# High weights first in a slab, low weights behind their own wait

## What is computed

```python
for i in range(2):                       # first model
    h = rmsnorm(x) ; proj = h @ w_in[i]  # attention, convolution and a state-space branch
    x = x + merged @ w_mix_o[i]
    gt, up = split(rmsnorm(x) @ w_ffn_in[i])
    x = x + (silu(gt) * up) @ w_ffn_out[i]
for l in range(2):                       # second model
    h = h + (sig(g1) * (yr @ ret_out[l]) + sig(g2) * (ys @ ssd_out[l])) @ w_o[l]
    h = h + (silu(gate) * up) @ w_down[l]
```

## Time and profile before

| | us |
|---|---|
| median of 3 runs (2136.08 to 2138.23) | 2136.47 |
| the profiled execution, its own time | 2139.59 |
| its span, first to last instruction | 2137.8 |
| PE busy | 2113.5 (99%) |
| DVE busy | 1640.1 (77%) |
| ACT busy | 1195.2 (56%) |

### The profile page before, as it was taken

How to read it: one execution, slowest core, us unless ns; L and a number is a source line. 1 busy time by engine, 2 the same in 40 slices (tenths; PEclk the granted TensorE clock), 3 DMA queues, 4 the chain that set the end, 5 groups by cost and what they waited for, 6 DMA issues and landing times.

```text
span 2137.8 us, 47790 instructions
## 1 busy us (share of the span) xinstructions
PE 2113.5 (99%) x18652; PEld 2055.5 (96%) x18652; DVE 1640.1 (77%) x2620; ACT 1195.2 (56%) x1803; POOL 58.5 (3%) x54
## 2 busy tenths in 40 slices
PE   9999999999999999999999999999999999999998
PEld 8999999999999999899999999999899999999998
DVE  8987877987877776778957877776678947877764
ACT  6646644565555445546648745445446658845443
POOL 0000000000000000000002200000000002200000
PEclk9999999999999999999999999999999999999999
DMA  7434655654446556554455566556554556565553
GB/s 251 159 128 141 204 190 186 195 171 142 151 157 215 190 189 206 187 168 158 161 190 191 167 203 208 186 187 213 185 169 148 169 183 193 174 201 186 187 189 127
DMA packets 109984, 385.00 MB, mean 180 GB/s; under 512 B 12480, under 2 KB 16768, under 8 KB 109312
## 3 DMA queue, kind: packets, MB, share of 16 engines
q1 hardware_dynamic: 101664, 368.66, 52.2%
q10 hardware_dynamic: 8160, 14.04, 2.1%
HBM read 381.53 MB, written 1.11 MB: 179 GB/s over the span
## 4 chain that ended last, share of the span: by engine, by line
PE 89%; DVE 6%; ACT 2%; issue 2%; DMA 0%; DVEq 0%; ACTq 0%
PE acc L777 25%; PE acc L779 24%; PE acc L778 24%; DVE w_lo L1811 2%; PE acc L896 1%; PE acc L897 1%; PE acc L898 1%; PE acc L841 1%; PE acc L843 1%; PE acc L842 1%; ACT w_hi L1310 1%; PE mid L1133 1%; PE mid L1214 1%; DVE pr L2564 0%; PE mid L964 0%
## 5 line engine op out<-in xcount | busy, mean ns | idle before, releaser
L1811 DVE TENSOR_TENSOR w_lo<-w_raw,w_hi 128x1024 fp32r<-128x1024 f32 x694 | 848.5, 1227 | 306.8 <-ACT w_hi L1310 297.9
L1310 ACT CAST w_hi<-w_raw 128x1024 fp32r<-128x1024 f32 x694 | 724.7, 1047 | 541.3 <-PE acc L779 473.5
L777 PE MATMUL acc<-h_hi,w_hi 128*128 128x256 f32 x2096 | 599.4, 286 | 0.3 <-DVE w_lo L1811 0.3
L779 PE MATMUL acc<-h_hi,w_lo 128*128 128x256 f32 x2096 | 587.5, 280 | 0.0
L778 PE MATMUL acc<-h_lo,w_hi 128*128 128x256 f32 x2096 | 586.3, 280 | 0.0
L777 PE MATMUL acc<-g_hi,w_hi 128*128 128x256 f32 x1456 | 410.0, 282 | 0.8 <-DVE w_lo L1811 0.7
L779 PE MATMUL acc<-g_hi,w_lo 128*128 128x256 f32 x1456 | 407.2, 280 | 0.0
L778 PE MATMUL acc<-g_lo,w_hi 128*128 128x256 f32 x1456 | 406.8, 279 | 0.0
L777 PEld LDWEIGHTS acc<-h_hi,w_hi 128*128 128x128 f32 x2096 | 395.7, 189 | 7.7 <-issue 5.7
L779 PEld LDWEIGHTS acc<-h_hi,w_lo 128*128 128x128 f32 x2096 | 396.1, 189 | 0.0
L778 PEld LDWEIGHTS acc<-h_lo,w_hi 128*128 128x128 f32 x2096 | 395.1, 188 | 0.5
(11 more groups left out here) (434 smaller groups left out, 3394.3 us busy)
## 6 DMA issues: line engine op xcount, KB each, us to landing
w_raw<-weights_d SPq DMA_DIRECT2D x695, 512.0 KB, 3.9
even<-rows_d ACTq DMA_DIRECT2D x16, 256.0 KB, 4.3
odd<-rows_d ACTq DMA_DIRECT2D x32, 128.0 KB, 3.4
p<-p_d ACTq DMA_DIRECT2D x3, 1080.0 KB, 8.5
rdec<-decay_d ACTq DMA_DIRECT2D x2, 768.0 KB, 5.3
p<-p_d SPq DMA_DIRECT2D x1, 1024.0 KB, 10.7
out_d<-work SPq DMA_DIRECT2D x4, 256.0 KB, 2.3
x_all<-x_d SPq DMA_DIRECT2D x1, 516.0 KB, 4.3
```

The source lines that it names most:

```text
L777: mm(dst, wh, hi[:, k, :], start=first and j == 0, stop=False)
L779: done = mm(dst, wl, hi[:, k, :], start=False, stop=last and j == len(ks) - 1)
L1310: nc.scalar.copy(w_hi[:, slot, :], w_raw[:, slot, :]).then_inc(hi_done, 1)
L1811: tt(w_lo[:, slot, :], w_raw[:, slot, :], w_hi[:, slot, :].bitcast(F32), SUB).then_inc(lo_v, 1)
```

## The change

`products` no longer makes the three matmuls of a block in turn. It first waits for ScalarE's cast (`hi_done`), does the two matmuls with the high weights for each k, then waits for VectorE's subtraction (`lo_v`), and does the eight matmuls with the low weights one after the other. The calls of `weights_of` in `slab_k8` and `slabs_long` go. The matmuls are the same and as many, and the waits `need` stay with the first loop.

```diff
                 slot = i % RING
+                pe.wait_ge(hi_done, at.slab + (i + 1))
                 for j, k in enumerate(ks):
                     if need is not None:
                         need(k)
-                    a = j * width + col
-                    wh, wl = w_hi[:, slot, a:a + P], w_lo[:, slot, a:a + P]
+                    wh = w_hi[:, slot, j * width + col:j * width + col + P]
                     mm(dst, wh, hi[:, k, :], start=first and j == 0, stop=False)
                     mm(dst, wh, lo[:, k, :], start=False, stop=False)
+                pe.wait_ge(lo_v, at.slab + (i + 1))
+                for j, k in enumerate(ks):
+                    wl = w_lo[:, slot, j * width + col:j * width + col + P]
                     done = mm(dst, wl, hi[:, k, :], start=False, stop=last and j == len(ks) - 1)
                 return done
...
             def slab_k8(at, i, t, need=None, hi=h_hi, lo=h_lo):
 
-                weights_of(at, i)
                 bank(at, t)
...
                         last_mean(0)
-                    weights_of(at, i + m)
                     ks = range(m * KD, min(m * KD + KD, blocks))
```

## The result

The changed kernel takes 2146.55 us (median of 5 runs, 2145.23 to 2148.08), the kernel before 2136.47: a ratio of 1.0043, with a 95% interval of 1.0032 to 1.0054. It is slower by 7 to 12 us. The forecast was 2147.7.

What follows compares the result with a forecast made beforehand. TensorE, busy 99%, was taken as the bound. The profiled 2139.6 us, -2.0 for waits and +13.2 for pace, gave 2150.8; the median lying 3.1 lower made it 2147.7 us, range 2132 to 2158.

Steps and rivals of the forecast that it cites:

- What bounds the kernel: TensorE, busy 99% of the span; one nanosecond in the matmuls' pace is 14.7 us, all low-weight waits a few us.
- The waits that go: Slab starts that waited for VectorE's subtraction now need the cast alone; pauses vanish, -4.1 us.
- The second `issue` at `r`: First slab on `r`: a pause listed under "issue" goes, 0.41 us, with the other layer's 0.8 us.
- The restart after a pause: Second matmul after a pause comes 0.20 us behind the first, not 0.12; some eight pauses gone give 0.6 us.
- The waits that grow: Slabs with late activations have more matmuls behind the last wait: `s` +1.5 us, `m` +0.6 us, `f` nothing.
- The pace: In `products`, eight low-weight matmuls in a row go slower than three in turn's 117.3 ns; the sixteen high ones keep it.
- The term of +13.2 us: Low-weight matmuls in `products`: 2.7 ns more for each of 4896 matmuls.
- The 120 ns: Pace of eight matmuls of high weights with `g_lo` ending `slab_raw`, taken for the eight low-weight matmuls in `products`.
- Rival 1: Order leaves the pace at 117.3 ns and waits alone decide: 2134.5 us, not slower; chance 0.38.
- Rival 2: Eight low-weight matmuls in a row go at 115 ns, as the 512-column rows: 2123 us, half of it 2129; chance 0.10.
- Rival 3: The sixteen high-weight matmuls slow to 118.1 ns too: 7.8 us more, 2155.5 us; shares the forecast's chance of 0.52.
- Rival 4: Low weights late by more than 1.88 us stop TensorE at the new mid-slab wait; given no chance of its own.

Runs made afterwards that it cites:

- e_three_rows: The changed kernel with three rows of eight matmuls per slab, and one common wait for eight matmuls of `slab_raw`; 2153.0 us, ratio 1.0060 to 1.0091.
- e_order: The changed kernel's matmul order, but with the old wait for `lo_v` in front of each slab and none in the middle; 2146.0 us, ratio 1.0027 to 1.0055.
- e_few: The kernel before with the changed order in only ten slabs, those whose low weights came late; 2137.1 us, ratio 0.9999.

## Why the prediction was right, and where it wasn't

**What bounds the kernel: right.** The pace of `products` decided. All waits together moved the time by less than a microsecond (-3.2 + 0.4 + 1.3 + 0.8 = -0.7), the pace by 8 to 9 (8.2 in the steps above; 14.7 ns x 612 slabs = 9.0). The total came nearer than its parts, and that is in part luck: the forecast had +11.2 us, the medians differ by 10.1, but pace and waits by the trace give 7.5 to 8.3. The pace was forecast 4 to 5 us too dear, the waits 1.3 us too cheap.

**The waits that go: -4.1 forecast, -3.2 measured, and 0.4 taken back.** The places were right. The second `issue` at `r` was right (-0.48 and -0.46 against 0.4). The restart after a pause and the small ones were counted too high.

**The waits that grow: right.** `s` +1.3 against +1.5, `m` +0.8 against +0.6, `f` nothing. The low part of `s` was itself made later than the working assumed, as everything before it was.

**The pace: the size nearly, the reason not.** The forecast was 118.2 ns and 761 matmuls in 90 us, the measurement 118.1 and 762; the eight low matmuls took 0.95 to 0.96 us, as forecast, and the sixteen kept 117.3 to 117.5. The term of +13.2 us was too big by 4 to 5: it took 2.7 ns more for each low matmul than three in turn, and 2.0 are measured (119.3 - 117.3). The 120 ns were read from times in hundredths of a us; with them a slab takes 2837 ns, but on `g`, where the loop was read, it takes 2832.8, on `h` 2830.6 and on `f` 2826.4. But the rule that I drew from the earlier trace rows, that the pace falls as the arrays alternate less, is wrong: rows of four (2815.4) lose nothing, and three rows of eight, the least alternation of all, cost only 3 ns a slab more than one. That the 120 ns of `slab_raw` nearly fitted the eight of `products` is luck as well: the rows of eight in e_three_rows go at 118.1. The step that failed was to make a rule of three paces that each stood for one order at one set of addresses.

**Rival 1, order doesn't touch the pace: fell.** e_order has the loads and matmuls of before and their waits, and is 15 ns a slab slower. The Trainium skill, "TensorE: Matmul & The Clock Gate", section "Step-by-step: what each phase is for", gives the two operands read ports of their own, so that loading weights takes nothing from the running matmul; that no order is slower, as I concluded from it, the traces here contradict: the order changes the pace by 0.5% (2816.0 to 2830.7 ns), the addresses by 0.5% (to 2830.4) and the start by 0.9% (2853 to 2827), and the measurement decides. What makes the patterns, in the reading of the operands or elsewhere, stays open.

**Rival 2, faster: not here,** though other orders of the same matmuls are (2807 ns in rows of two). **Rival 3, the pairs lose too: no;** the sixteen go as before. **Rival 4: not seen.** The 0.6 us of line 782 stand at slab 30, but its low weights had long been there (the second line is its first low matmul):

```profile
95.28 1.22 DVE L1812 TENSOR_TENSOR w_lo<-w_raw,w_hi 128x1024 fp32r<-128x1024 f32 x1
...
114.53 1.22 PE L782 MATMUL acc<-h_hi,w_lo 128*128 128x256 f32 x8 [0.38 <-issue]
```

In e_few TensorE stands for 0.8 us behind as many matmuls of the same slab, three in turn, where no wait is. What holds it there stays open.

**The own time of the profiled run.** The 3.1 us that I took off were right to take off: after's profiled run lies on its median, and 1.4 us of the 3.1 stand between slabs 29 and 46, in the stretch at the lower clock.

## What to carry to other kernels

Where one engine is busy for 99%, cost a new order by the pace of that engine first: one nanosecond a matmul was worth more here than all the waits that the change removed. Read that pace as the time of a whole group of matmuls, slab by slab, and look whether it takes a few separate values; if so, a pace from another order, another array or another stretch is only a guess, and two or three orders (rows of two, of four) and a shift of operands by 32 bytes are cheap to try. A wait that is taken away for one operand only pays up to the next late one, so look at what comes right behind it.

## What the runs showed of the hardware

- The 24 matmuls of a slab, in the same order, mostly take one of a few times, within 2 ns: on `h` 2807, 2826 or 2853 in rows of two, 2827, 2831 or 2853 three in turn with moved arrays; 2833, 2829 or 2827 with low weights last. A stretch keeps its value or, as in the kernel before, goes through the same five values over and over; one slab at its head in another order moved all three stretches of 4 to 17 slabs behind it from 2853 to 2827.
- Low operands moved from 48 to 16 bytes behind a multiple of 64 (and some arrays by whole multiples of 64) made three in turn 14 ns a slab slower (2816.0 to 2830.4): 10 us for the kernel without one instruction moved.
- Behind a pause of TensorE at 102 to 106 us the granted clock was 0.50 until 108 in the profiled run of after, and into 110 to 112 in that of before; in that of e_order it stayed at 1.00. Slab 29 alone ends 1.3 to 3.5 us earlier against its neighbours in the other kernels' traces than in that of before, so this stretch may make a part of the scatter of 2 to 7 us in the totals. It isn't all of it: the profiled run of e_order, with the full clock here, is the slowest of its five (2149.74 us).
